# Mixture-of-experts block: expert sums kept in four row sets in place of two

## The reference, cut to what matters

```
def _moe_routed(h, idx, wts, wg, wu, wd):
    ...
    def step(acc, blk):
        tok, w, e = blk
        xb = h_pad[tok]
        y = (jax.nn.silu(xb @ wg[e]) * (xb @ wu[e])) @ wd[e]
        return acc.at[tok].add(y * w[:, None].astype(y.dtype)), None
...
        f = _moe(tokens, ...)            # routed experts + shared expert
        x = x + g2 * _rms_norm(f[:n_lat].reshape(bsz, s_len, dm), post_ffn_g[l])
```

## Time and profile before

| | |
|---|---|
| time before, median of 3 runs | 3179.77 us (3175.15 to 3190.14) |
| the profiled execution, its own time | 3172.14 us |
| its span in the trace | 3170.3 us |
| PE busy | 2724.0 us, 86% of the span |
| DVE busy | 1233.7 us, 39% |
| POOL busy | 1093.0 us, 34% |
| POOL's own transfer queue | 87.63 MB |
| SP's transfer queue | 530.30 MB |
| granted clock of PE over the span | 0.923 |

### The profile page before, as it was taken

One profiled execution on the slowest core, in us unless ns is written; L12 is line 12 of the kernel. 1 busy time (PEld: TensorE's weight loads), 2 busy tenths in 40 slices (PEclk: granted clock), 3 DMA queues, 4 the chain that ended last, 5 costly groups with the idle time before them and its releaser, 6 DMA issues. The chain is left out here.

```text
span 3170.3 us, 44086 instructions
## 1 busy us (share of the span) xinstructions
PE 2724.0 (86%) x13025; PEld 1417.8 (45%) x13026; DVE 1233.7 (39%) x3418; ACT 563.2 (18%) x1258; POOL 1093.0 (34%) x952
## 2 busy tenths in 40 slices
PE   6688988997969999999998378899977989899894
PEld 5364746663623333333333256666743333333331
DVE  5653544343333333333333664452533223233223
ACT  2131322221001111111111221321310111111111
POOL 0674977921002212212212273677310112112111
PEclk9888998998789999999999789899988999999997
DMA  6120122211367998999994411032124899998993
GB/s 223 35 82 22 47 93 92 60 47 64 121 240 235 342 329 285 305 317 316 315 361 158 161 40 57 27 93 92 48 99 167 322 374 389 367 388 288 374 336 100
DMA packets 193651, 619.22 MB, mean 195 GB/s; under 512 B 23440, under 2 KB 117904, under 8 KB 160016
## 3 DMA queue, kind: packets, MB, share of 16 engines
q1 hardware_dynamic: 159856, 530.30, 44.2%
q0 software_dynamic: 33696, 87.63, 11.5%
HBM read 578.84 MB, written 77.99 MB: 207 GB/s over the span
## 5 line engine op out<-in xcount | busy, mean ns | idle before, releaser
L1436 PE MATMUL ps<-wgu,xT 128*64 128x512 f32 x3584 | 818.9, 611 | 57.7 <-DMA wgu<-in_exp_gu 52.0
L1372 POOL DMA_INDIRECT ffn_rows<-Y,six x114 | 182.3, 1599 | 1161.8 <-issue 783.5
L1436 PEld LDWEIGHTS ps<-wgu,xT 128*64 128x64 f32 x3584 | 258.0, 140 | 523.8 <-issue 521.8
L1446 PE MATMUL ps<-wd,hiddenT 128*64 128x512 f32 x1824 | 422.9, 605 | 13.5 <-issue 12.5
L546 PE MATMUL ps<-w_in,hT 128*128 128x512 f32 (+3 forms) x1152 | 394.1, 502 | 15.7 <-PEq L481 4.3
L1595 DVE TENSOR_TENSOR hidden<-silu,ps 128x256 f32<-128x256 f32 x112 | 47.2, 421 | 731.1 <-ACT silu L1535 731.1
L546 PEld LDWEIGHTS ps<-w_in,hT 128*128 128x128 f32 x1152 | 212.3, 202 | 183.0 <-issue 175.1
L1446 PEld LDWEIGHTS ps<-wd,hiddenT 128*64 128x64 f32 x1824 | 130.8, 138 | 226.2 <-issue 224.1
L1535 ACT ACTIVATE silu<-ps 128x256 f32<-128x256 f32 x112 | 43.1, 385 | 825.4 <-PE ps L1436 818.8
L1589 DVE TENSOR_SCALAR Y<-ps,wc 128x512 f32<-128x512 f32 x114 | 85.6, 751 | 205.8 <-PE ps L1446 205.8
L1421 PE MATMUL ps<-cst,X 128*128 128x128 f32 x912 | 126.3, 282 | 37.9 <-DMA X<-h_rows,gix 20.0
(11 more groups left out here) (456 smaller groups left out, 3782.9 us busy)
## 6 DMA issues: line engine op xcount, KB each, us to landing
wgu<-in_exp_gu SPq DMA_DIRECT2D x128, 2048.0 KB
wd<-in_exp_d SPq DMA_DIRECT2D x128, 1024.0 KB
ada_start<-in_ada_w SPq DMA_DIRECT2D x8, 1024.0 KB, 9.8
w_in<-in_w_in SPq DMA_DIRECT2D x4, 2048.0 KB, 8.5
w_in<-in_w_out SPq DMA_DIRECT2D x4, 2048.0 KB, 10.4
aw_0A<-in_ada_w SPq DMA_DIRECT2D x12, 512.0 KB, 3.8
aw_0B<-in_ada_w SPq DMA_DIRECT2D x12, 512.0 KB, 3.9
w_in<-in_w_in SPq DMA_DIRECT2D x2, 3072.0 KB, 10.6
```

The source lines that it names most:

```text
L1372: pool.indirect_dma_start(out=v.acc_dram, out_offset=bass.IndirectOffsetOnAxis(ap=six[j][:, 0:1], axis=0), in_=Y[j][:, :], in_offset=None, ...
L1436: last = pe.matmul(ps[h * HB:(h + 1) * HB, 0, :], xT[:, k, h * HB:(h + 1) * HB], wgu[w[h]][:, k, :], start=(k == 0), stop=(k == KD - 1))
L1446: last = pe.matmul(ps[h * HB:(h + 1) * HB, 1 + c, :], G[:, f, h * HB:(h + 1) * HB], wd[w[h]][:, f, c * 512:(c + 1) * 512], start=(f == 0), ...
```

## The change

`ffn_rows` becomes two tensors, `ffn_rows0` and `ffn_rows1`, each with the two sets of NROW rows: a pass of one parity adds into one pair of sets, a pass of the other parity into the other pair. `added` becomes two counts. The scatter of pass i no longer waits for that of pass i-1; after it and after the gather, POOL waits until the scatter of pass i-1 has landed, and raises `y_free` only then. All of the second pair but the last tile of its second set has to be zeroed in `route` too, and `ffn_residual` reads and adds four sets.

```
 (route, SP)
                 s_clear.wait(sp, 3)
+                for i in range(nt):
+                    sp.dma_start(v.acc_dram[1][i * P:(i + 1) * P, :], ex.Y[0][:, :]).then_inc(s_zero.sem, 16)
                 for i in range(nt - 1):
-                    sp.dma_start(v.acc_dram[NROW + i * P:NROW + (i + 1) * P, :], ex.Y[0][:, :]).then_inc(s_zero.sem, 16)
+                    for j in range(U):
+                        sp.dma_start(v.acc_dram[j][NROW + i * P:NROW + (i + 1) * P, :], ex.Y[0][:, :]).then_inc(s_zero.sem, 16)
...
 (experts, POOL)
                 def scatter(j):
-                    pool.sem_inc(y_free, 1)
-                    pool.indirect_dma_start(out=v.acc_dram, ...
+                    pool.indirect_dma_start(out=v.acc_dram[j], ...
-                                            compute_op=ALU.add).then_inc(added, 16)
+                                            compute_op=ALU.add).then_inc(added[j], 16)
-                def body(i, j):
+                def body(i, turn, j):
                     before = 1 - j
                     pool.wait_ge(y_act, i + (1 + CREDIT))
                     pool.wait_ge(y_dve, i + (1 + CREDIT))
                     pool.wait_ge(y_index, i + 1)
-                    pool.wait_ge(added, i * 16 + 16)
+                    waited()
                     scatter(before)
...
                     gather(before)
+                    pool.wait_ge(added[j], turn * 16 + (16 + 16 * j))
+                    pool.sem_inc(y_free, 1)
...
-                pool.dma_start(v.acc_dram[NROW + (nt - 1) * P:NROW + nt * P, :], Y[0][:, :]).then_inc(added, 16)
+                for j in range(U):
+                    pool.dma_start(v.acc_dram[j][NROW + (nt - 1) * P:NROW + nt * P, :], Y[0][:, :]).then_inc(added[j], 16)
                 for b in range(2):
                     pool.wait_ge(index, b + 1)
                     gather(b)
+                pool.wait_ge(added[0], 16)
+                pool.wait_ge(added[1], 16)
                 pool.sem_inc(y_free, 1)
...
 (ffn_residual, SP and DVE)
-                    sp.dma_start(f[:, i, :], v.acc_dram[i * P:(i + 1) * P, :]).then_inc(s_f[i].sem, 16)
-                    sp.dma_start(f2[:, i, :], v.acc_dram[NROW + i * P:NROW + (i + 1) * P, :]).then_inc(s_f[i].sem, 16)
+                    for q in range(2 * U):
+                        rows = slice(q % 2 * NROW + i * P, q % 2 * NROW + (i + 1) * P)
+                        sp.dma_start(parts[q][:, i, :], v.acc_dram[q // 2][rows, :]).then_inc(s_f[i].sem, 16)
...
-                    s_f[i].wait(dve, 32)
-                    dve.tensor_tensor(f[:, i, :], f[:, i, :], f2[:, i, :], ALU.add).then_inc(s_sum.sem, 1)
+                    s_f[i].wait(dve, 64)
+                    dve.tensor_tensor(f[:, i, :], f[:, i, :], parts[1][:, i, :], ALU.add)
+                    step(dve.tensor_tensor(parts[2][:, i, :], parts[2][:, i, :], parts[3][:, i, :], ALU.add))
+                    dve.tensor_tensor(f[:, i, :], f[:, i, :], parts[2][:, i, :], ALU.add).then_inc(s_sum.sem, 1)
```

More of the change, by code:

```diff
@@ L119, in build @@
         h2_dram = nc.dram_tensor("h2_rows", (NROW, HROW), F32, kind="Internal").ap()
-        acc_dram = nc.dram_tensor("ffn_rows", (2 * NROW, D), F32, kind="Internal").ap()
+        acc_dram = [nc.dram_tensor(f"ffn_rows{j}", (2 * NROW, D), F32, kind="Internal").ap() for j in range(U)]
         env = dict(nc=nc, t=t, S=S, sb=sb, ps=ps, banks=banks, xs=xs, cst=cst, csth=csth, small=small, mods=mods,
@@ L1031, in _ @@
                     s_yd.wait(sp, i + 1)
-                    sp.dma_start(v.acc_dram[i * P:(i + 1) * P, :], Y[:, i % 2, :]).then_inc(s_ys[i % 2].sem, 16)
+                    sp.dma_start(v.acc_dram[0][i * P:(i + 1) * P, :], Y[:, i % 2, :]).then_inc(s_ys[i % 2].sem, 16)
                 for j in range(2):
@@ L1037, in _ @@
                 s_ws.wait(sp, 16)
-                s_zero.wait(sp, 16 * (nt - 1))
+                s_zero.wait(sp, 16 * (3 * nt - 2))
             @block.gpsimd
@@ L1264, in route @@
                  (s_si, len(work)), (s_g, len(work)), (s_dn, nt), (s_ya, nt), (s_yd, nt), (s_ys[0], 8 * nt), (s_ys[1], 8 * nt),
-                 (s_clear, 3), (s_zero, 16 * (nt - 1)), (s_sel, 1), (s_cnt, 1), (s_nb, 1), (s_slot, 1), (s_tab, 1), (s_tt, 1)):
+                 (s_clear, 3), (s_zero, 16 * (3 * nt - 2)), (s_sel, 1), (s_cnt, 1), (s_nb, 1), (s_slot, 1), (s_tab, 1), (s_tt, 1)):
         s.stage_over(k)
@@ L1285, in experts @@
     down, y_act, y_dve, y_index = sem("down"), sem("y_by_act"), sem("y_by_dve"), sem("y_index")
-    added, step_s = sem("added"), sem("expert_step")
-    pool_waited, y_free = sem("pool_waited"), sem("y_free")
+    added, step_s = [sem("added0"), sem("added1")], sem("expert_step")
+    pool_waited, y_free = S("pool_waited").sem, sem("y_free")
     CREDIT = 1
@@ L1316, in loop @@
                             for j in range(U):
-                                body(turn * U + j, j)
+                                body(turn * U + j, turn, j)
         def entry(eng, column, i, hi):
@@ L1370, in scatter @@
                 def scatter(j):
[L1371 to L1372 removed]
+                    pool.indirect_dma_start(out=v.acc_dram[j], out_offset=bass.IndirectOffsetOnAxis(ap=six[j][:, 0:1], axis=0),
                                             in_=Y[j][:, :], in_offset=None, bounds_check=2 * NROW - 1, oob_is_err=False,
[L1374 to L1376 removed]
+                                            compute_op=ALU.add).then_inc(added[j], 16)
+                def body(i, turn, j):
                     before = 1 - j
@@ L1404, in _ @@
                 pool.wait_ge(y_index, turns16 // 8 + 1)
-                pool.wait_ge(added, turns16 * 2 + 16)
+                waited()
                 scatter(1)
-                pool.wait_ge(added, turns16 * 2 + 32)
+                pool.wait_ge(added[0], turns16 + 16)
+                pool.wait_ge(added[1], turns16 + 32)
                 pool.wait_ge(gathered[0], turns16 + 32)
@@ L1642, in ffn_residual @@
         f = v.sb(f"f{l}", [P, nt, D], scope=scope)
-        f2 = v.sb(f"second{l}", [P, nt, D], scope=scope)
+        parts = [f, *(v.sb(f"part{q}_{l}", [P, nt, D], scope=scope) for q in range(1, 2 * U))]
         g2 = v.sb(f"g2_{l}", [P, streams, D], scope=scope)
@@ L1699, in ffn_residual @@
     for s in s_f:
-        s.stage_over(32)
+        s.stage_over(64)
     s_sum.stage_over(nt)
```

## The result

The changed kernel takes 3204.23 us (median of 7 runs, 3196.57 to 3214.49) against 3180.9 (3175.15 to 3190.14) for the kernel before in the same comparison: ratio 1.0076, 95% interval 1.0052 to 1.0099. It is slower. The forecast was 3214, with a range of 3199 to 3228.

A forecast was written before the change was run, and what follows sets the result against it. PE was taken to bound layer 0, and layer 1 with stretches of late weights. Terms -2 + 0 + 0 + 6 + 30.5 = +34.5 us on a median of 3179.77 gave 3214 us, range 3199 to 3228.

The forecast's parts named there:

- the landing was not what PE waited for, and the ends of both layers pay: The main forecast for the whole kernel: 3214 us, range 3199 to 3228, chance 0.78.
- The scatter's wait goes behind the gather: POOL in both loops: scatter and gather issued up to 2.4 us sooner in 24 passes; gain 2 us, bounds 0 and 20.
- ffn_residual: Block after each layer's loop: twice the loads, three adds for one; cost 17.8 and 12.7 us, together 30.5, bounds 15.8 and 49.
- The 16.2 us without a releaser: Layer 0's loop: 23 short PE waits ahead of the transposes, 16.2 us, forecast to stay within some us.
- the rival that said so: Layer 0's loop: the 16.2 us are late-landing rows and go with sooner gathers; gain 20 us, 3196 us, chance 0.10.
- `y_free` comes later: DVE's row index needs the scatter landing two passes back; about 20.6 us allowed, 6 to spare, cost 0.
- More zeros in route: SP issues 11 more 512 KB stores in layer 0 and 7 in layer 1; idle DMA engines have room, cost 0.
- Two zero stores ahead of the first gather: POOL's queue before each loop: the second store delays the first gather 3 us a layer, 6 in all; bounds 0 and 10.4.
- The weights come sooner: Layer 1's loop: `wgu` loads get the DMA engines when needed; all 52.0 us of waits gone gives 3162 us, chance 0.03.
- A new wait: Loops: landings may exceed 20.6 us, so DVE, ACT, then PE stop for `y_free`; 3262 us, chance 0.06.
- Signs that would prove me wrong: Either loop over 10 us shorter, DVE's row index waiting for `y_free`, or residual's extra loads much faster than 2.63 us a pair.
- the 5 that I allowed: Both layers' loops: forecast to keep their lengths within 5 us.

The follow-up runs named there:

- experiment 1: Changed kernel with four row sets zeroed, read and added, but every scatter into the first pair behind the one before: 3209.97 us, 1.0108; again 3214.94 us, 1.0118.
- the other three serial traces: Traces with one scatter at a time: the kernel before run again (3175.9 us) and two executions of the changed kernel with scatters serial into the first pair (1.0108, 1.0118).
- the repeats: Both kernels run again unmodified: the changed kernel 3201.28 us, 1.0067; the kernel before 3175.9 us, 0.9991.
- the repeat of before: The kernel before, run again with nothing changed: 3175.9 us, 0.9991.
- the costs alone: Changed kernel keeping all four row sets' zeroing, loads and adds, but scatters one behind the other into the first pair: 3209.97 us, then 3214.94 us.
- experiment 6: Kernel before, order kept, five small GpSimd pow operations put ahead of the scatter in each pass: 3165.17 us, 0.9958.
- experiment 7: Changed kernel with four row sets, the gather issued ahead of the scatter in each pass: 3176.38 us, 0.9996.
- experiment 4: Kernel before, two row sets and one scatter at a time, the gather issued ahead of the scatter and its wait: 3144.0 us, 0.9882.

## Why the prediction was right, and where its sum was off

The sign, the range and the mechanism of the loss held: the landing was not what PE waited for, and the ends of both layers pay.

- *The scatter's wait goes behind the gather, gain 2 us.* This is the mis-sized term. By the medians of experiment 1 it is 10 to 16 us, by the traces 5.9. I counted the 2.0 us of waits for X in layer 0 and took the 2.0 in layer 1 as 0. One trace's count was also low: the other three serial traces have 5.1 to 6.1 us over both loops. The change came out at +23.3 us where the sum has +34.5. Of these 11.2 us the traces place 7: 3.9 in this term, 1.7 in the first gathers and 1.3 in ffn_residual. The other 4 have no place in a trace; they may be this term by the medians, or spread.
- *The 16.2 us without a releaser.* Right that they would stay (16.3), and right that they are not late X's: the rival that said so gave 3196 and falls. But I didn't ask what they were, and they held the larger prize: with them gone the kernel is 1.2% faster.
- *`y_free` comes later, 0.* Held: landings up to 13.5 us, 20.6 allowed, no wait.
- *More zeros in route, 0.* Held, with a wrong detail: SP was held 18.4 us, not 8.3. The cover, 38 us until its next transfer, was large enough.
- *Two zero stores ahead of the first gather, 3 and 3.* 2.5 and 1.8, and 1.6 and 1.6 in the repeats.
- *ffn_residual, 17.8 and 12.7.* 17.2 and 12.0. The landings and DVE's 6.1 us a tile came as worked out. From tile 1 to tile 2 four loads took 5.19 us, 2.60 a pair: the row's 2.63 and not the 2.4 by the fit that the prediction takes from the Trainium skill (DMA: Bandwidth & Descriptors, Anatomy of one DMA). The page gives that fit for transfers issued from GpSimd, and these are SP's. DVE is busy 28.9 us more (1262.6 for 1233.7), where 23 was forecast: 20 adds of 1.22 us on their own rows are 24.4. The last 4.5 are within what differs anyway: the repeats have 1259.9 and 1237.4.
- *The weights come sooner.* No: 57.3 us of waits for `wgu` in the change, 52.0 before, 55.0 in the repeat of before. *A new wait:* none.
- *Signs that would prove me wrong.* None showed. Layer 0's loop shortened by 4.8 us (6.2 in the mean of two traces of each kernel, just over the 5 that I allowed), below 10.

Open: how a scatter slows the read. What the traces narrow it to is the time just behind the scatter's issue. In the six traces of before, the change and the costs alone, 296 of 672 reads take over 2.4 us, and 284 of these start 0.5 to 3.0 us after a scatter's issue. A scatter issued beside the read (experiments 6 and 7) doesn't slow it, nor does one in flight since 8 us (experiment 4's pass). Whether it is the scatter's descriptors, its reads of Y or its first rows in HBM, no run here parts. Not every read with such a scatter is slow either: in layer 0 of before 38 of 51 take over 2.4 us. That the read is 0.85 us in some passes and 2.2 in most is not explained.

## What to carry to other kernels

A wait that is long on its own engine is worth what the last engine in the chain loses by it; here 244 us of POOL's were 6 of PE's by the traces, and the ends of the block, which nothing covered, cost 34. Before paying for more buffers to free a transfer from the one ahead, try the order of issue on that queue: it is free, and it gave 37 us where the buffers lost 23. But look at what the order moved. Here it was not mainly the earlier gather, whose waits for X were 4 us, but the scatter, which no longer came 2 us ahead of a read on PE's path; experiment 6 gets 17 of layer 0's 24 us with the order kept. And short waits with "issue" as releaser, always at the same instruction, are worth a look at what the sequencer does just ahead of it, here a read of a table.

## What the runs showed of the hardware

A read of nine numbers from SBUF by PE's sequencer takes 2.2 us in most passes of experiments 4, 6 and 7. With an accumulating indirect scatter of 128 rows issued 1.4 to 1.75 us into the products, some 2 us ahead of the read, 38 of 51 reads in layer 0 of the kernel before took over 2.4 us, up to 4.05 (4.27 in the changed kernel). With the scatter moved away from there, in those three kernels, no read in that layer's loop took over 2.4. The Trainium skill, SBUF — State Buffer, section SBUF: two separate sides, says that engine ports and DMA ports cannot contend with each other. By that page alone a transfer would not slow an engine's access; these reads are slowed, and no run here shows by which side a sequencer's read goes. 16 stores of 512 KB held SP for 18.4 us where 5 held it for 2.62.
